# A two-layer decoder trunk: sums of weight blocks made by adding DMAs instead of by VectorE

## What is computed

```python
D_MODEL = 1024; SEQ = 512; D_FF = 4 * D_MODEL
def squared_relu_mlp(h, w_up, w_down):
    a = jax.nn.relu(h @ w_up)
    return (a * a) @ w_down
for layer in range(2):
    x = x + rmsnorm(mix(rmsnorm(x, g[0])), g[1])
    x = x + rmsnorm(squared_relu_mlp(rmsnorm(x, g[2]), w_up, w_down), g[3])
```

## Time and profile before

| what | value |
|---|---|
| median of 3 runs | 1075.75 us (1074.98 to 1076.94) |
| the profiled execution's own time | 1075.44 us |
| its span, first to last instruction | 1073.6 us |
| PE busy | 1056.8 us, 98% of the span |
| DVE, ACT, POOL busy | 748.7, 538.6, 189.3 us |
| DMA: bytes moved, mean rate | 99.94 MB, 93 GB/s |

### The profile page before, as it was taken

The page is one execution under the profiler, slowest core; times in us unless marked ns, Lnnn a source line. Parts: engine busy times, 40 slices in busy tenths (PEclk is TensorE's granted clock), DMA queues, the critical chain, the costliest instruction groups (busy, mean ns, idle before and its releaser), DMA issues.

```text
span 1073.6 us, 14865 instructions
## 1 busy us (share of the span) xinstructions
PE 1056.8 (98%) x5408; PEld 859.5 (80%) x5408; DVE 748.7 (70%) x1286; ACT 538.6 (50%) x1016; POOL 189.3 (18%) x333
## 2 busy tenths in 40 slices
PE   9999999999999999999999999999999999999997
PEld 8877779888888888888778766679888888888886
DVE  5455636596697696687589898526596696696685
ACT  6677645253453453425554567745254443453422
POOL 0464320000000000005413387520000000000005
PEclk9999999999999999999999999999999999999999
DMA  9531505544535445422613333006553535535402
GB/s 301 115 79 41 118 1 133 123 100 97 115 82 118 105 92 118 96 62 53 140 36 79 79 79 80 1 1 144 112 111 86 118 79 118 115 82 118 106 12 79
DMA packets 52009, 99.94 MB, mean 93 GB/s; under 512 B 4704, under 2 KB 4832, under 8 KB 51936
## 3 DMA queue, kind: packets, MB, share of 16 engines
q1 hardware_dynamic: 51216, 98.61, 40.4%
q10 hardware_dynamic: 720, 0.38, 0.1%
HBM read 96.88 MB, written 2.10 MB: 92 GB/s over the span
## 4 chain that ended last, share of the span: by engine, by line
PE 91%; DVE 5%; issue 1%; ACT 1%; DMA 1%; POOL 0%; DVEq 0%; POOLq 0%; SPq 0%; ACTq 0%
PE bank L2062 11%; PE bank L2060 11%; PE bank L2061 11%; PE bank L2437 7%; PE bank L2435 7%; PE bank L2436 7%; PE bank L2070 6%; PE bank L2072 6%; PE bank L2071 6%; PE bank L2219 3%; PE bank L2461 2%; PE bank L2460 2%; PE bank L2459 2%; PE bank L2288 2%; PE bank L2274 2%
## 5 line engine op out<-in xcount | busy, mean ns | idle before, releaser
L2060 PE MATMUL bank<-r_hi,w_hi 128*128 128x512 f32 (+1 forms) x456 | 177.5, 389 | 0.0
L2061 PE MATMUL bank<-r_hi,w_lo 128*128 128x512 f32 (+1 forms) x456 | 177.4, 389 | 0.0
L2062 PE MATMUL bank<-r_lo,w_hi 128*128 128x512 f32 (+1 forms) x456 | 177.4, 389 | 0.0
L1651 DVE TENSOR_TENSOR w_lo<-w_raw,w_hi 128x1024 fp32r<-128x1024 f32 x84 | 102.0, 1222 | 70.9 <-ACT w_hi L1170 70.7
L1170 ACT ACTIVATE w_hi<-w_raw 128x1024 fp32r<-128x1024 f32 x84 | 88.0, 1056 | 119.4 <-PE bank L2062 82.9
L2435 PE MATMUL bank<-w_hi,hid_hi 128*128 128x512 f32 x336 | 130.7, 389 | 0.0
L2436 PE MATMUL bank<-w_lo,hid_hi 128*128 128x512 f32 x336 | 130.7, 389 | 0.0
L2437 PE MATMUL bank<-w_hi,hid_lo 128*128 128x512 f32 x336 | 130.7, 389 | 0.0
L1179 ACT ACTIVATE w_hi<-w_raw,gT 128x512 fp32r<-128x512 f32 x96 | 64.5, 716 | 106.6 <-DMA w_raw<-in_w_mlp_up 75.1
L814 POOL TENSOR_TENSOR acc<-acc,G 128x512 f32<-128x512 f32 x8 | 13.0, 1651 | 594.3 <-ACT waste L1026 594.3
L2062 PEld LDWEIGHTS bank<-r_lo,w_hi 128*128 128x128 f32 (+1 forms) x456 | 85.2, 187 | 18.2
(11 more groups left out here) (215 smaller groups left out, 2149.4 us busy)
## 6 DMA issues: line engine op xcount, KB each, us to landing
w_raw<-in_w_mlp_up SPq DMA_DIRECT2D x64, 512.0 KB, 6.4
w_raw<-in_w_mlp_down SPq DMA_DIRECT2D x64, 512.0 KB, 6.9
w_raw<-in_b_w_in SPq DMA_DIRECT2D x16, 512.0 KB, 6.8
w_raw<-in_a_w_in SPq DMA_DIRECT2D x8, 512.0 KB, 9.3
w_raw<-in_a_w_out SPq DMA_DIRECT2D x8, 512.0 KB, 5.8
w_raw<-in_b_w_out SPq DMA_DIRECT2D x8, 512.0 KB, 6.0
xt<-in_x_turned SPq DMA_DIRECT2D x8, 256.0 KB, 4.9
X<-in_x SPq DMA_DIRECT2D x4, 512.0 KB, 11.1
```

The source lines that it names most:

```text
L1651: nc.vector.tensor_tensor(half_of(w_lo[:, u % 2, :], a), b_of(PRODUCTS[i][1], a), half_of(w_hi[:, u % 2, :], a).bitcast(f32), ALU.subtract ...
L2060: nc.tensor.matmul(bank, whi, xhi, start=start, stop=False)
L2061: nc.tensor.matmul(bank, wlo, xhi, start=False, stop=False)
L2062: return nc.tensor.matmul(bank, whi, xlo, start=False, stop=stop)
```

## The change

T1 to T4 of the six quarters are no longer made by DVE. All four become plain sums, so that a DMA which adds to its destination can make them: T1 = B11 + B12, T2 = T1 + B22, T3 = B22 + B12, T4 = B21 + T2. `weight_sums` on POOL issues two adding DMAs for each sum, of 64 partitions each, in the order T1, T2, T3, T4. For T1 to T3 the addend is read from `w_down` in HBM, for T4 from the place of T2 in SBUF; the destination is the raw place of the first term. SP no longer loads B12; in its stead it loads B22 a second time, into the place of T3. ACT now waits for a whole sum where it waited for the half that it splits. The signs of S1, S4 and of three of the totals follow. The number of DMAs that SP issues stays the same, and POOL issues 48 in all. The SBUF area for descriptors of such DMAs grows from 1024 to 2048 bytes of a partition; for its sake the two small tables `rope_t` and `rope_u` move into the space of `yg`.

```diff
-T_ORDERED = ("T1", "T2", "T4")
+T_ORDERED = ("T1", "T2")
-        offset = [1280]
+        offset = [2304]
...
-        rope_t, rope_u = at("rope_t", [8, ROT], f32, offset[0]), at("rope_u", [8, ROT], f32, offset[0] + 512)
-        offset[0] += 1024
+        rope_t, rope_u = at("rope_t", [8, ROT], f32, yg_at), at("rope_u", [8, ROT], f32, yg_at + 512)
...
+        def t_of(layer, q, name):
             if name == "T3":
-                return t3_made, 2 * quarter_no(layer, q) + a + 1
+                return t3_made, 32 * quarter_no(layer, q) + 32
+            if name == "T4":
+                return t4_made, 32 * quarter_no(layer, q) + 32
+            return t_made, 64 * quarter_no(layer, q) + 32 * T_ORDERED.index(name) + 32
...
                     fetch_up(n, 1)
-                    sp.wait_ge(*t_of(layer, q, "T1", 1))
-                    sp.wait_ge(*t_of(layer, q, "T3", 1))
+                    if q:
+                        sp.wait_ge(b_lo_done, part_no(layer, q - 1, 6, 1))
                     fetch_down(q, "B21")
...
                         fetch_down(n, "B22")
-                        sp.wait_ge(*t_of(layer, q, "T4", 1))
+                        sp.wait_ge(*t_of(layer, q, "T4"))
                         fetch_down(n, "B11")
                         sp.wait_ge(*low_of(up_unit(layer, n, 3)))
                         fetch_up(n + 1, 0)
-                        sp.wait_ge(b_lo_done, part_no(layer, q, 6, 1))
-                        fetch_down(n, "B12")
+                        sp.wait_ge(b_lo_done, part_no(layer, q, 5, 1))
+                        fetch_t3(n)
...
+            def added(name, src, done):
+                dst = raw(B_PLACE[name]).rearrange("p (k n) -> p k n", k=4)
+                for a in range(2):
+                    rows = slice(64 * a, 64 * a + 64)
+                    nc.gpsimd.dma_start(dst[rows], src[rows], accum_op=ALU.add).then_inc(done, 16)
+            def weight_sums(layer, q):
+                pool.wait_ge(b_lo_done, part_no(layer, q, 0, 1))
+                added("T1", down_block(layer, q, "B12"), t_made)
+                pool.wait_ge(b_lo_done, part_no(layer, q, 1, 1))
+                added("T2", down_block(layer, q, "B22"), t_made)
+                pool.wait_ge(*loaded((layer, q, "T3")))
+                added("T3", down_block(layer, q, "B12"), t3_made)
+                pool.wait_ge(b_lo_done, part_no(layer, q, 4, 1))
+                added("T4", raw(B_PLACE["T2"]).rearrange("p (k n) -> p k n", k=4), t4_made)
...
                 if name[0] == "T":
-                    act.wait_ge(*t_of(layer, q, name, a))
+                    act.wait_ge(*t_of(layer, q, name))
...
-            def weight_sum(layer, q, name, a):
...
-            def t3_sum(layer, q):
...
-                    if q:
-                        t3_sum(layer, q)
-                        for a in range(2):
-                            weight_sum(layer, q, "T1", a)
...
-    nc = bacc.Bacc("TRN2", target_bir_lowering=False, num_devices=1, dynamic_dma_scratch_size=1024)
+    nc = bacc.Bacc("TRN2", target_bir_lowering=False, num_devices=1, dynamic_dma_scratch_size=2048)
```

More of the change, by code:

```diff
@@ L87, in mlp_role @@
     return what, q + (what == "up"), n
-B_PLACE = {"B12": 0, "T1": 1, "B21": 0, "T4": 0, "B11": 1, "T2": 1, "B22": 2, "T3": 3}
+B_PLACE = {"T1": 1, "B21": 0, "T4": 0, "B11": 1, "T2": 1, "B22": 2, "T3": 3}
 DOWN_PLACE = (2, 1, 3, 0)
@@ L99, in raw_loads @@
         order += [(up_unit(layer, 0, n), n % 2) for n in range(UPS)]
-        order += [((layer, 0, "B22"), 2), (up_unit(layer, 1, 0), 4), ((layer, 0, "B12"), 0), ((layer, 0, "B11"), 1)]
+        order += [((layer, 0, "B22"), 2), ((layer, 0, "T3"), 3), ((layer, 0, "B11"), 1), (up_unit(layer, 1, 0), 4)]
         for q in range(LAST):
@@ L104, in raw_loads @@
             if n < LAST:
-                order += [((layer, n, "B22"), 2), ((layer, n, "B11"), 1), (up_unit(layer, n + 1, 0), 4), ((layer, n, "B12"), 0)]
+                order += [((layer, n, "B22"), 2), ((layer, n, "B11"), 1), (up_unit(layer, n + 1, 0), 4), ((layer, n, "T3"), 3)]
             else:
@@ L662, in fetch_up, with fetch_t3 @@
                     fetch(up_unit(layer, q, n), up_source(q, n))
+                def fetch_t3(q):
+                    fetch((layer, q, "T3"), down_source(q, 1, 1))
                 def fetch_down(q, b):
@@ L670, in load_mlp @@
                 fetch_down(0, "B22")
-                sp.wait_ge(*low_of(up_unit(layer, 0, 2)))
-                fetch_down(0, "B12")
+                sp.wait_ge(pv_done, PT_AT[16 * (layer + 1)])
+                fetch_t3(0)
                 sp.wait_ge(*low_of(up_unit(layer, 0, 3)))
@@ L927, in _ @@
                 x_squares(layer)
+                for q in range(LAST):
+                    weight_sums(layer, q)
             for j in range(NB):
@@ L1658, in hidden_sum @@
                     dve.wait_ge(*s_of(layer, q, "S3", a))
-                    args = a_of("S1", a), a_of("A21", a), a_of("A22", a), ALU.add
+                    args = a_of("S1", a), a_of("A21", a), a_of("A22", a), ALU.subtract
                 elif name == "S2":
@@ L1667, in hidden_sum @@
                         dve.wait_ge(a_lo_done, part_no(layer, q - 1, 3, a))
-                    args = a_of("S4", a), a_of("A12", a), a_of("S2", a), ALU.subtract
+                    args = a_of("S4", a), a_of("A12", a), a_of("S2", a), ALU.add
                 nc.vector.tensor_tensor(*args).then_inc(s_made, 1)
-            def weight_sum(layer, q, name, a):
[L1673 to L1687, removed]
             def s3_sum(layer, q):
@@ L1720, in totals @@
                 dve.wait_ge(part_out, part_tile(layer, LAST, 0, 0))
-                for n, (out_, a, b, op) in enumerate(((2, 0, 2, ALU.add), (5, 2, 5, ALU.add), (2, 2, 1, ALU.add), (3, 3, 2, ALU.add),
-                                                      (1, 1, 5, ALU.add), (2, 5, 6, ALU.subtract), (0, 0, 4, ALU.add))):
+                for n, (out_, a, b, op) in enumerate(((2, 0, 2, ALU.add), (5, 2, 5, ALU.add), (2, 1, 2, ALU.subtract), (3, 3, 2, ALU.add),
+                                                      (1, 1, 5, ALU.subtract), (2, 5, 6, ALU.add), (0, 0, 4, ALU.add))):
                     if n:
@@ L1787, in mlp @@
                     a_lows(q, 1)
-                    for a in range(2):
-                        b_low(layer, q, 1, a)
-                        weight_sum(layer, q, "T2", a)
+                    b_lows(q, 1)
                     for a in range(2):
@@ L1813, in mlp @@
                     a_lows(q, 6)
-                    for a in range(2):
-                        b_low(layer, q, 4, a)
-                        weight_sum(layer, q, "T4", a)
+                    b_lows(q, 4)
                     up_split(layer, n, 3, range(4))
```

23 lines of the change are left out of this document (7 added, 16 removed).

## The result

The median is 1079.43 us (9 runs, 1077.56 to 1079.8) against 1076.15 us of the kernel before: a ratio of 1.0025, 95% interval [1.0015, 1.0036]. The interval lies wholly above 1: the change makes the kernel slower, by about a quarter of a per cent. The forecast was no change, 1075.7 us.

A forecast was written before the change was run, and what follows sets the result against it. The prediction took PE as the bound, busy 1056.8 of 1073.6 us. Profiled execution 1075.44 - 0.2 at most + 0 = 1075.4 us, with 0.3 more for a median: 1075.7 us, range 1074 to 1092.

The forecast's parts named there:

- What bounds the kernel, and what DVE's relief is worth: In the six quarters PE is the bound, lacking 0.22 us; removing 57.6 us of DVE work per quarter is worth 0.
- What an adding DMA takes: Each sum on POOL: 10 us from issue to landing, between 7.3 at the low end and 17 at the high end.
- The prediction's other estimate: For each sum, an add lands after 2.6 + 1.93 x 4.7 = 11.7 us, by the skill page's rule.
- The larger area for descriptors changes no instruction's length: Layout: the larger descriptor area and the moved tables change no instruction's length.
- How long T2 may take: From product 1's low parts, T2 may take 16.1 us before PE's start of product 2 is late.
- the prediction's 328.1: Second quarter of layer 0: time by which T2 must land, 2.3 us before PE starts product 2 at 330.40.
- T1 and T4: In each quarter T1 may take 16.9 us and T4 14.8 us; at 10 us each they cost 0.
- Rival A: T3's add slows up 2's load on shared DMA engines: 7 to 38 us slower, say 1086 us; chance 0.25.
- 335 GB/s: Rate read in slices where two transfers overlap, against 220 for one load; the reason for pricing shared engines at 0.
- Rival B: Adds take some 20 us, POOL slow or held up in issuing: 7 us a quarter, 42 in six, 1118; chance 0.12.
- What would show it: Signs in the profile after: PE busy throughout each quarter and adds landing in 8 to 12 us if right; others for rivals.
- the sign given for B: In the quarters: PE waits at the products, and ACT's splits of T1 and T2 are ended by the adding DMA.

The follow-up runs named there:

- e1: The changed kernel with each sum made by one adding DMA of 128 partitions in place of two of 64: 1075.86 us, ratio 0.9998.
- e4: The changed kernel with a descriptor area of 1024 bytes in place of 2048: 1082.13 us, ratio 1.0053.
- e10: The changed kernel with its adds issued on POOL in the order T1, T3, T2, T4, still in two halves: 1076.6 us, ratio 1.0004.
- e5: The changed kernel run again, unaltered, beside runs of the kernel before: 1080.43 us, ratio 1.0035.
- e3: The kernel before with the layout edits alone (2048-byte descriptor area, tables moved), no adding DMAs: 1075.98 us, ratio 0.9999.
- e6: The changed kernel with T4 made by four adding DMAs of 128x512 in place of two: 1080.95 us, ratio 1.0044.
- e7: The changed kernel, but POOL issues T3's adds only when product 2's low parts are made: 1079.37 us, ratio 1.0026.
- e2: The changed kernel with T2 alone made by one adding DMA of 128 partitions, the other sums in two halves: 1075.76 us, ratio 0.9996.
- e8: e1, but POOL clears a spare table 36 times before it issues T2: 1075.7 us, ratio 1.0.

## Why the prediction was wrong, point by point

- **What bounds the kernel, and what DVE's relief is worth:** right. e1 has DVE 54 us less busy, and the time of before.
- **What an adding DMA takes:** this step failed. 10 us was nearly right for one sum whose halves go out together or in one (T1 8.9 us; T2 11.5 in e1, of which 4.1 passed before its data moved, behind a load). The prediction's other estimate, 11.7 us by the ratio of 1.93 of the Trainium skill, page "Collectives: The Full Stack", section "The bandwidth ceiling: the fold count and why AG ≠ RS ≠ AR", was too high for an add by itself: T1 in e1, 1.05 MB with next to no load beside it, landed in 8.6 to 8.7 us. But the forecast priced T2 like T1, as one transfer. It is two in series here, 17.9 to 20.1 us from the low parts' end, where 10 were put in.
- **"The larger area for descriptors changes no instruction's length":** beside the point. I priced this edit at nothing and did not ask what the area limits. It limits how many adds are out: e4 moves the hold by this number alone.
- **How long T2 may take:** 16.1 us was too short; 18.6 is measured. Counted from PE's start of product 0, product 1's low parts end 4.3 us earlier than before in the second quarter (10.0 us after it, 14.2 before), not "a little earlier", so T2's time begins that much sooner. It also ends sooner, at 28.9 us and not at the 30.3 that the prediction's 328.1 amounts to, because I named no queue behind ACT's wait for T2, as I had for T1. The first to be late is not product 2 but up 2 and its hidden tiles, behind T2 in ACT's order; product 2 itself lost 0.3 us, in one quarter.
- **T1 and T4:** right; they cost nothing in the changed kernel. The 16.9 us allowed for T1 were too many, though: in e4 it took 14.3 to 15.6 us from product 0's low parts in four quarters, and they lost 0.2 to 1.7 us.
- **Rival A, shared engines:** its effect is there. Up 2's two loads took 7.1 us in the median in the second quarter (5.6 before), but they were issued 2.8 us earlier (319.21 against 322.02 in the earlier trace rows). The wait behind a load lengthens each half of T2, but without the hold it costs nothing: e1. The reason I gave for pricing it at nothing was a misreading: 335 GB/s stands in single slices of half a us, once at the start of up 2's load with nothing beside it, and while up 1 and B21 moved together the other slices show 191 to 250, no more than one load's rate.
- **Rival B, late sums:** the nearest to what happened, at chance 0.12. Its "some 20 us" and "held up in issuing" were right; what holds POOL up is the adds still out, not DVE: every hold ends about 0.3 us behind a landing. Its price was wrong: 7 us a quarter, 42 in six, where 0 to 1.5 and 3.0 were lost, because T1 is not late and T2 only by what exceeds its room.
- **What would show it:** the sign given for B, ACT's split of T2 ended by the adding DMA, is the row that showed it; PE's wait came at up 2, where I had looked for A.

Open are two things. First, the rule of the hold. In the changed kernel T2's second half waits for the first although T1's halves had landed by 307.06, before T2 was issued at 310.82; in e10 T3's second half went out at 303.98, when T1 had landed, with T3's first half still out until 306.7. No count of places that I tried gives both. One rule does, found in the traces when all runs were in, and it fits each of the 414 adds of the ten kernels that have them, the 82 that were held and the 332 that were not. The area of 2048 bytes has room for three halves of T1 to T3 and not for four, a half of T4 counted at half of one (1024 bytes have half that room); when the room is used up, POOL waits until everything issued so far on the semaphore of the oldest add on its list has landed, and then strikes all of these off. T1 and T2 count on one semaphore, `t_made`, so T2's second half waits for T2's first although T1 is long in; in e10 the oldest are T1's halves, nothing later is out on `t_made`, and T3's second half goes when T1 has landed. Two simpler rules, to wait for the oldest add or for all that are out, fail for at least 34 adds. But the rule is a fit: no run gave T2 a semaphore of its own, which by it would move the hold to T3's second half, and what part of the system waits in this way is not shown. Second, the start: 1.2 us late in the changed kernel, 3.2 in e5, 1.1 in e4, but not in e3, e6, e7 or e10. e5's median lies 4.1 us above before, of which its quarters explain 2.8. Whether the rest is scatter or belongs to the program was not settled.

No version beat the kernel before: PE has no more than 0.2 us to gain in these stretches, and e1, e2, e8 and e10 all come out at its time.

## What to carry to other kernels

When work moves to another way of issuing it, ask how many of the new items can be out at once, and which one in the order is the first that has to wait; put an item there that nobody needs soon, or make fewer and larger ones. For every delivery, follow the queue of the engine that waits for it: the first loser is often what stands behind the wait, not the consumer of the delivery. A late delivery costs only what exceeds its room, so price it from a limit, quarter by quarter, and not as a constant times all quarters.

## What the runs showed of the hardware that I had not expected

- An adding DMA issued by POOL can be held, without any wait in the program, until earlier ones have landed; in the changed kernel this was 7 to 10.5 us, six times of six. It goes on about 0.3 us after a landing. With 1024 bytes of a partition for descriptors, one add of 64 partitions of 4 x 512 floats is out at a time; with 2048, up to three.
- Such an add of 512 KB that travels alone lands in 5.5 to 6.2 us (e4), one of 1 MB in 8.6 to 8.7 (T1 in e1): doubling the bytes adds some 3 us. With loads or other adds ahead of them the same adds take 8 to 14 us; in e1's second quarter T2's data started 4.1 us after its issue, behind B21's load, and T1's 2.0 us after its own.
- An add of 512 KB occupies POOL for 1.0 us, one of 1 MB for 1.3.
